# Sparse-attention layer: in blocks 8 to 14 the next head's first three logits pieces are issued before the wait for this head's exponentials

## The reference, cut to what matters

```python
rel = jnp.einsum('bqhd,bsd->bqhs', iqb, ik)                 # index score, 8 small heads
score = jnp.einsum('bqh,bqhs->bqs', iwb, jax.nn.relu(rel))
score = jnp.where(key_pos[None, None, :] <= t[None, :, None], score, -jnp.inf)
_, sel = lax.top_k(score, k_top)                            # k_top = 256
logits = jnp.einsum('bqhr,bqkr->bqhk', qb, kv_sel) * (R_KV ** -0.5) + bias    # 4 heads
p = jax.nn.softmax(logits, axis=-1)
return jnp.einsum('bqhk,bqkr->bqhr', p, kv_sel)
```

## Time and profile before

| what | value |
|---|---|
| time, median of 3 runs | 4161.95 us (4160.95 to 4162.1) |
| time of the profiled execution | 4160.26 us |
| its span | 4158.4 us |
| PE busy | 3865.9 us, 93% |
| DVE busy | 2670.4 us, 64% |
| ACT busy | 1364.9 us, 33% |
| last layer, by its first and last row of DVE's maximum | from 2894.0 to 4116.9 us |

### The profile page before, as it was taken

One profiled execution on the slowest core, in us unless ns is written; L12 is line 12 of the kernel. 1 busy time (PEld: TensorE's weight loads), 2 busy tenths in 40 slices (PEclk: granted clock), 3 DMA queues, 4 the chain that ended last, 5 costly groups with the idle time before them and its releaser, 6 DMA issues. The chain is left out here.

```text
span 4158.4 us, 59840 instructions
## 1 busy us (share of the span) xinstructions
PE 3865.9 (93%) x23339; PEld 2688.2 (65%) x23339; DVE 2670.4 (64%) x4970; ACT 1364.9 (33%) x2906; POOL 924.1 (22%) x544
## 2 busy tenths in 40 slices
PE   8999999998999999987999999998899989998877
PEld 5556555665666666656888888886566656665544
DVE  5656565655777767753566555663456777778874
ACT  1222222221111111112333333332344545555552
POOL 1444433442233223321222222221000000000000
PEclk9999999999999999989999999999999999999988
DMA  7343434333544444441000000022100010000000
GB/s 262 127 148 122 147 122 147 130 129 123 188 147 137 138 144 148 139 155 42 24 27 22 27 22 25 17 79 83 36 24 31 19 36 19 19 18 19 18 13 18
DMA packets 197087, 342.12 MB, mean 82 GB/s; under 512 B 20213, under 2 KB 100426, under 8 KB 196682
## 3 DMA queue, kind: packets, MB, share of 16 engines
q1 hardware_dynamic: 196810, 338.26, 23.2%
HBM read 298.90 MB, written 39.33 MB: 81 GB/s over the span
## 5 line engine op out<-in xcount | busy, mean ns | idle before, releaser
L249 PE MATMUL e_ps<-arena 128*128 128x386 f32 (+1 forms) x1960 | 653.8, 487 | 5.7 <-DMA arena<-l_w_in 3.3
L249 PEld LDWEIGHTS e_ps<-arena 128*128 128x128 f32 x1960 | 364.7, 191 | 250.1 <-issue 19.0
L249 PE MATMUL o_ps<-arena 128*128 128x320 f32 x1624 | 461.9, 436 | 18.6 <-DVE o_hh L321 5.1
L1630 PE MATMUL d_ps<-hT_in,arena 128*128 128x128 f32 x3072 | 393.4, 283 | 13.4 <-ACT hT_in L1849 11.4
L249 PEld LDWEIGHTS o_ps<-arena 128*128 128x128 f32 x1624 | 301.1, 191 | 147.4 <-issue 13.8
L1630 PEld LDWEIGHTS d_ps<-hT_in,arena 128*128 128x128 f32 x3072 | 360.6, 193 | 29.0 <-ACT hT_in L1849 12.6
L2375 PE MATMUL s_ps<-hT_in,arena 128*128 128x128 f32 x2016 | 239.9, 279 | 0.0
L2375 PEld LDWEIGHTS s_ps<-hT_in,arena 128*128 128x128 f32 x2016 | 236.5, 196 | 3.0 <-issue 2.0
L2657 PE MATMUL s_ps<-s_w_out,arena 128*128 128x512 f32 x512 | 228.3, 600 | 0.0
L1154 PE MATMUL o_ps<-o_w_out,o_gt 128*128 128x512 f32 x512 | 225.7, 599 | 0.0
L640 PE MATMUL e_ps<-e_w_out,e_gt 128*128 128x512 f32 x512 | 223.7, 595 | 0.0
(11 more groups left out here) (510 smaller groups left out, 6925.4 us busy)
## 6 DMA issues: line engine op xcount, KB each, us to landing
arena<-l_w_in SPq DMA_DIRECT2D x48, 1024.0 KB, 7.8
arena<-l_w_in SPq DMA_DIRECT2D x32, 1040.0 KB, 8.3
xb<-x SPq DMA_DIRECT2D x64, 512.0 KB, 4.3
arena<-l_w_in SPq DMA_DIRECT2D x16, 1544.0 KB, 9.5
arena<-l_w_in SPq DMA_DIRECT2D x16, 1280.0 KB, 7.4
arena<-l_w_in SPq DMA_DIRECT2D x32, 504.0 KB, 6.9
arena<-l_w_in SPq DMA_DIRECT2D x16, 768.0 KB, 7.0
o_scratch<-w_ada SPq DMA_DIRECT2D x16, 768.0 KB
```

The source lines that it names most:

```text
L249: m = pe.matmul(bank[(g + k) % 2][:, 0:self.n], rows[:, kk * P:(kk + 1) * P], cols[:, kk, :], start=(kk == 0 and k in (0, 1, 4)), stop=(kk ...
L1630: m = pe.matmul(bank[c % 2][:, t * P:(t + 1) * P], W_in[:, k, (4 * c + t) * P:(4 * c + t + 1) * P], hT[:, k * P:(k + 1) * P], start=(k == ...
```

## The change

A constant `LEAD_FROM = 8` replaces `BLOCKS - 1` (15) in the condition that decides how many logits pieces of the next head stand before the wait. Blocks 8 to 14 get `lead = 3`; block 15 had it, blocks 0 to 7 keep 0. Nothing is added or removed: per head 0 to 2 of these seven blocks the three pieces move ahead of the wait and of the transposes of this head's piece 0, and the fourth piece (blocks 12 to 14) moves from c = 3 to c = 0 of the loop over the pieces.

```diff
+LEAD_FROM = 8
...
-                    lead = min(3, n_pieces) if i >= BLOCKS - 1 else 0
+                    lead = min(3, n_pieces) if i >= LEAD_FROM else 0
                     for c in range(lead):
                         logits(h + 1, c)
                     pe.wait_ge(*exp_ready.upto(i, h + 1))
```

## The result

The changed kernel takes 4188.6 us (median of 4 runs, 4184.75 to 4190.96), the kernel before 4161.9 us. The ratio is 1.0065, with a 95% interval of 1.0049 to 1.0081: slower by 0.65%, or 26.7 us. The profiled execution of the changed kernel took 4184.75 us, its span is 4182.9 us.

A forecast was written before the change was run, and what follows sets the result against it. PE, busy 93%, was taken as the bound, with the DVE-ACT bisection chain nearly as long within heads. Losses of 7.1 + 7.2 + 7.8 + 3.6 = 25.7 us gave 4188 us, range 4175 to 4199.

The forecast's parts named there:

- The circle: Blocks 12 to 14: DVE rounds, first read, PE, ACT's copy and rounds in series; block 12's first turn +3.75 us.
- the 2 to 6 foretold: PE's waits in us at the logits line for DVE's read, three in each of blocks 12 to 14.
- The turns of the four-piece blocks: Blocks 12, 13 and 14: turns from head to head lengthen, reaching +7.1, +7.2 and +7.8 us per block.
- The clock: PE at half speed after the first stall of blocks 12 to 14: 1.4 us each, 2.2 more in block 14.
- The three-piece blocks: Blocks 8 to 11: no fourth piece blocks, ACT's chain comes later; +1.7, +0.7, 0 and +1.2, together +3.6 us.
- The rival that ended faster: Pieces fill PE's waits for exponentials in blocks 8 to 14, nothing blocks: 14 us gained, 4148 us; chance 0.06.
- No change: Stalls fall where PE waited anyway, blocks 12 and 13 nearly free: within 8 us of 4162; chance 0.06.

The follow-up runs named there:

- Experiment 3: Changed kernel, but in blocks 8 to 14 the fourth piece is issued at c = 3 again; 4161.83 us against 4161.27 for the kernel before.
- Experiment 4: Changed kernel, but in blocks 12 to 14 DVE reads the next head's first piece before its last round; 4164.77 us against 4161.27 for the kernel before.
- Experiment 8: Change in blocks 12 to 14 only, plus 4, 4 and 5 unused matmuls in head 0's stall; 4179.5 us against 4160.84 for the kernel before.
- experiment 2: Change in blocks 12 to 14 only, other blocks as in the kernel before; 4187.56 us against 4161.27 for the kernel before, ratio 1.0062.
- Experiment 6: Kernel before with one piece ahead in blocks 12 to 14, next piece's transposes before the logits piece; 4151.74 us against 4160.84, ratio 0.9977.
- Experiment 1: Change in blocks 8 to 11 only, blocks 12 to 14 as in the kernel before; 4164.37 us against 4161.27, ratio 1.0009.
- experiment 5: Kernel before with one piece ahead of the wait in blocks 12 to 14 only; 4154.89 us against 4160.84, ratio 0.9985.
- experiment 7: Kernel before with three pieces ahead in blocks 12 to 14, next piece's transposes before the fourth piece; 4174.64 us against 4160.84, ratio 1.0031.

## Why the prediction was right

4188 was forecast and 4188.6 measured, inside the range of 4175 to 4199. That the two agree to a microsecond is luck: by the marks of the profiled executions the blocks lost 30.3 us and not 25.7, nearly all of the difference in the four-piece blocks, while the medians are 26.7 apart and the same code differs by some us between executions. The steps are the better test.

- **The circle.** The first stall of block 12 was put at 3.5 us and is 3.43; the second at 2.2 and is 2.24. ACT's first round was to start 5.2 us later and came, with the 2.1 us allowed for by which this execution was ahead at block 12, 5.5 us later (3809.52 + 2.1 - 3806.10). Of the nine waits two, in the last turns of blocks 12 and 13, are 1.58 and 1.77 us, a little under the 2 to 6 foretold. Experiments 3 and 4 cut the circle at either end, and the loss of blocks 12 to 14 went from 26 us to 1.7 and 5.1.
- **The turns of the four-piece blocks.** For block 12, 5.2 + 0.7 + 1.2 us were forecast and 5.5 + 1.0 + 1.3 came; for block 13, 5.7 + 0.5 + 1.0 against 6.0 + 1.0 + 1.0; for block 14, 4.7 + 1.3 + 1.8 against 6.1 + 1.1 + 1.8. The one term clearly too small is block 14's first turn: I had taken 1.4 us of loss by the half clock there, as in block 10, and after a stall of 6.18 us the half clock held on longer. The granted clock was 0.50 from 4027 to 4033 us, and from the fourth piece (4027.34) to ACT's round (4034.44) it is 7.10 us, where the sum had 4.3 at full clock: 2.8 us by the clock and not 1.4. In addition, 0.3 to 0.5 us per block behind the heads, and 0.4 ahead of them in block 13, was taken as nothing. Together the terms of these blocks were 22.1 us and the trace has 26.4: each of the three came out 1.1 to 1.7 us longer than its sum.
- **The clock.** 1.4 us per first stall and 2.2 more in block 14 is 6.4 us. Experiment 8 against 2 gives 6.1 by blocks (28.0 less 21.9) and 7.6 by medians, but that is no confirmation of the term: only 4.3 of the 6.1 us are first turns of blocks 12 and 13, and 2.0 are later parts of block 14, in which both kernels issue the same and which differ between executions. Against the changed kernel's trace, which has the same code in these blocks as experiment 2, it is 4.5 us. So the clock is shown to cost PE time behind these stalls, some 1.6 us in the first turns of blocks 12 and 13 against that trace; the whole is known only to lie about between 4.5 and 7.6 us.
- **The three-piece blocks.** 1.7, 0.7, 0 and 1.2 were forecast; 1.78, 0.86, -0.09 and 1.30 came. The turns are less well explained than the totals: in each of these blocks the turn from head 2 to head 3 is 1.0 to 1.2 us longer. Block 10 is at nothing because its two turns before that are 1.3 us shorter, not because the pieces are free there; its half clock behind head 0 is gone, as forecast (granted clock 1.00 from 3609 to 3613 us, 0.50 behind the wait before).
- **The rival that ended faster** held half of what it said. The gaps were filled: PE's waits for exponentials fell by 18.4 us, more than the 14 that it counted on. The Trainium skill, Perfetto Trace Analysis, section Identifying Performance Opportunities, sends one to the gaps of the most-contended engine and has what they wait for start sooner; here these gaps closed, the engine's busy share stayed at 93%, and the time rose. Experiment 6 shows that the advice isn't wrong: in blocks 12 to 14 pieces issued earlier can win 9 us, if the work put there doesn't hold up what another engine waits for.
- **No change** failed by its condition: only block 14 had idle time where the stall fell, and it lost most of all, since its price wasn't PE's time but ACT's rounds.

Left open: the changed kernel's runs spread over 6.2 us, those of experiment 2 over 1.5, with four runs each, and why isn't known beyond what stands in the last section. Two pieces ahead, and one piece ahead in blocks 8 to 11, were not run.

## What to carry to other kernels

Before work is moved ahead of a wait on an in-order engine, look at the last instruction of it, not at the first: the buffer that it needs decides, and whatever stands behind it inherits that wait. Price the stall by who waits for what is queued behind it; here waits of 31 us went with a cost of 14 us in one order, and waits of 34 us with 26 in another. If the next-but-one buffer is freed by an engine that is itself waiting for this queue, the move closes a circle; here one piece ahead was faster than none, and three were slower than none.

## What the runs showed that I hadn't expected

PE's clock makes identical code take different times in different executions. In block 10, which experiment 2 leaves as it was, PE waits 3.17 us for head 0's exponentials, as before. In its trace:

```profile
3613.20 1.08 PE L2592 MATMUL s_ps<-ident,s_Lg 128*128 128x128 f32 x4 [3.17 <-ACT s_Lg L2734]
3614.08 1.91 PE L2582 MATMUL s_ps<-arena 128*128 128x512 f32 x2
3615.78 1.06 PE L2592 MATMUL s_ps<-ident,s_Lg 128*128 128x128 f32 x4
```

The second set of transposes takes 1.06 us here and took 0.67 in the trace before, so the half clock lasted longer behind the same gap (from 3617 to 3619 us the granted clock was 0.50 here and 1.00 before), and head 1's exponentials come 1.6 us later. Experiment 1 has the same in block 14, which it doesn't touch: 2.0 us. The profiled executions start block 7's exponentials up to 7.8 us apart, 3.6 of which are there 120 us into the span. Of the six us by which the changed kernel's execution came earlier to block 8, 3.2 arise in block 4, which both kernels run alike: at its start the granted clock was 0.53 before (3133 to 3142 us) and 0.88 in the changed kernel's trace (3130 to 3138 us). So the one gap of block 10 cost 1.4 us in one execution and, as an estimate (1.4 + 1.6), 3.0 in another; what decides between them isn't shown. A comparison of totals of single executions is no better than that. The table by block, which takes differences of near marks, repeats to within 0.04 us in most untouched blocks from 6 on, but not in all: block 12 is 0.4 us longer in experiment 1, block 8 is 0.4 shorter in experiments 5 and 7, and block 15 is 1.6 shorter in five of the nine traces.
